# GpSimd subtracts each quarter of a weight unit in four instructions of 256 columns instead of one of 1024

## What is computed

```
x = first_block(x)        # rms norm, projections of x @ w_in (1024 x 9728),
                          # three dilated window attentions, retention in two
                          # directions, gated merge, w_out; then a mixture of 64
                          # experts (group top 1, expert top 2); final rms norm
for l in range(2):        # second_block
    h = rmsnorm(x, g_pre_mix[l])
    y = token_mixer(h, w_in[l], ...)      # mLSTM (4 heads) and window attention (8 heads), w_out
    x = x + rmsnorm(y, g_post_mix[l])
    h = rmsnorm(x, g_pre_ffn[l])
    y = conv_ffn(h, w_up[l], ffn_conv_w[l], w_down[l])   # up to 2 x 2816, conv of 3, gate, down
    x = x + rmsnorm(y, g_post_ffn[l])
```

## Time and profile before

| what | us |
|---|---|
| median of 3 runs (2905.0 to 2905.14) | 2905.1 |
| span of the profiled execution, first to last instruction | 2908.4 |
| TensorE busy | 2679.7 |
| VectorE busy | 1321.1 |
| ACT busy | 873.5 |
| GpSimd busy | 691.6 |

### The profile page before, as it was taken

The page is one execution under the profiler, slowest core; times in us unless marked ns, Lnnn a source line. Parts: engine busy times, 40 slices in busy tenths (PEclk is TensorE's granted clock), DMA queues, the critical chain, the costliest instruction groups (busy, mean ns, idle before and its releaser), DMA issues.

```text
span 2908.4 us, 35516 instructions
## 1 busy us (share of the span) xinstructions
PE 2679.7 (92%) x14188; PEld 1911.4 (66%) x14188; DVE 1321.1 (45%) x2407; ACT 873.5 (30%) x1643; POOL 691.6 (24%) x306
## 2 busy tenths in 40 slices
PE   7999999999988888888888789999999999899998
PEld 7997877888533333333333267788888777788887
DVE  4333745314733333333333367464443564744433
ACT  3333333423211111111111134543333334433332
POOL 4233232542000000000000122224544222144443
PEclk9999999999999999999999989999999999999999
DMA  3222211234999999999999921122232221122321
GB/s 143 87 88 91 91 66 37 102 118 188 380 427 427 428 428 429 429 428 429 429 428 428 382 86 38 50 81 94 87 115 88 85 95 59 58 87 87 94 110 73
DMA packets 126800, 572.19 MB, mean 197 GB/s; under 512 B 10704, under 2 KB 58192, under 8 KB 101328
## 3 DMA queue, kind: packets, MB, share of 16 engines
q1 hardware_dynamic: 121424, 561.08, 48.6%
q10 hardware_dynamic: 5248, 9.32, 1.0%
HBM read 566.12 MB, written 4.26 MB: 196 GB/s over the span
## 4 chain that ended last, share of the span: by engine, by line
PE 63%; DMA 25%; DVE 7%; ACT 3%; issue 1%; POOL 1%; POOLq 0%; SPq 0%; ACTq 0%; DVEq 0%
PE ps L344 39%; DMA wide<-in_moe_w 17%; PE ps L1264 8%; DMA arena<-in_moe_w 6%; PE ps L1692 4%; PE ps L1676 3%; PE ps L569 2%; PE ps L1062 1%; PE ps L540 1%; ACT ring_r L299 1%; PE ps L555 1%; DMA ring<-in_w_in 1%; DMA ring<-in_w_up 1%; POOL ring_r L313 1%; PE ps L1053 1%
## 5 line engine op out<-in xcount | busy, mean ns | idle before, releaser
L313 POOL TENSOR_TENSOR ring_r<-ring,ring_r 128x1024 fp32r<-128x1024 f32 (+1 forms) x280 | 676.7, 2448 | 2138.1 <-ACT ring_r L299 2138.1
L344 PE MATMUL ps<-xnT_r,ring_r 128*128 128x512 f32 (+1 forms) x1664 | 488.2, 376 | 3.4 <-DVE xn_r L2580 2.1
L344 PE MATMUL ps<-ring_r,xnT_r 128*128 128x512 f32 (+1 forms) x1360 | 447.8, 401 | 10.4 <-POOLq L255 5.0
L344 PEld LDWEIGHTS ps<-xnT_r,ring_r 128*128 128x128 f32 x1664 | 306.4, 190 | 63.4 <-POOL ring_r L313 3.4
L344 PE MATMUL ps<-ring_r,arena_r 128*128 128x512 f32 x1392 | 329.3, 394 | 0.0
L344 PEld LDWEIGHTS ps<-ring_r,xnT_r 128*128 128x128 f32 x1360 | 290.9, 226 | 56.4 <-issue 11.6
L344 PE MATMUL ps<-xn_r,ring_r 128*128 128x512 f32 (+1 forms) x832 | 311.9, 375 | 0.0
L344 PEld LDWEIGHTS ps<-ring_r,arena_r 128*128 128x128 f32 x1392 | 261.9, 190 | 58.9 <-issue 4.9
L299 ACT ACTIVATE ring_r<-ring 128x1024 fp32r<-128x1024 f32 (+2 forms) x284 | 270.7, 1024 | 90.2 <-DMA ring<-in_w_down 69.1
L1676 PE MATMUL ps<-wide,arena 128*32 128x512 f32 x1536 | 199.4, 642 | 99.5 <-DMA wide<-in_moe_w 99.0
L1676 PEld LDWEIGHTS ps<-wide,arena 128*32 128x32 f32 x1536 | 42.0, 112 | 236.0 <-DMA wide<-in_moe_w 143.4
(11 more groups left out here) (359 smaller groups left out, 3762.7 us busy)
## 6 DMA issues: line engine op xcount, KB each, us to landing
wide<-in_moe_w SPq DMA_DIRECT2D x144, 2048.0 KB, 27.6
arena<-in_moe_w SPq DMA_DIRECT2D x48, 2048.0 KB, 27.4
ring<-in_w_in SPq DMA_DIRECT2D x25, 2048.0 KB, 8.2
ring<-in_w_up SPq DMA_DIRECT2D x22, 2048.0 KB, 8.6
ring<-in_w_down SPq DMA_DIRECT2D x10, 2048.0 KB, 7.9
ring<-in_w_out SPq DMA_DIRECT2D x6, 2048.0 KB, 8.3
ring<-in_w_ret_branch SPq DMA_DIRECT2D x2, 2048.0 KB, 8.8
attn_spill<-arena ACTq DMA_DIRECT2D x2, 1056.0 KB, 7.3
```

What stands on the lines that cost most here:

```text
L313: nc.gpsimd.tensor_tensor(ring_r[:, q % 2, cols], ring[:, q % 2, cols], ring_r[:, 2 + q % 2, cols].bitcast(F32), ALU.subtract).then_inc(ha ...
L344: ins = nc.tensor.matmul(bank, left, right, start=(start and k == 0), stop=(stop and k == 2))
```

## The change

`low_pool` no longer issues one subtraction for a quarter but four, each over a fourth of its columns (256 of 1024, 132 of 528, 128 of 512). The wait for ACT stays ahead of the first, and only the last counts `half_low` up, so that TensorE waits for the same counts as before.

```diff
+        LOW_PIECES = 4
+
         def low_pool(pool, q):
             if current["l"] is not None and q == Q_UP + 1:
                 pool.wait_ge(half_low, quarter_count(Q_UP, 3))
             for part in range(2 if current["l"] is not None and q == Q_UP else 4):
                 cols = unit_quarter(q, part)
                 pool.wait_ge(half_high, quarter_count(q, part))
-                nc.gpsimd.tensor_tensor(ring_r[:, q % 2, cols], ring[:, q % 2, cols], ring_r[:, 2 + q % 2, cols].bitcast(F32),
-                                        ALU.subtract).then_inc(half_low, 1)
+                n = (cols.stop - cols.start) // LOW_PIECES
+                for at in range(cols.start, cols.stop, n):
+                    piece = slice(at, at + n)
+                    ins = nc.gpsimd.tensor_tensor(ring_r[:, q % 2, piece], ring[:, q % 2, piece], ring_r[:, 2 + q % 2, piece].bitcast(F32),
+                                                  ALU.subtract)
+                ins.then_inc(half_low, 1)
```

## The result

The changed kernel takes 2884.7 us (median of 4 runs) against 2905.05: a ratio of 0.9929, with a 95% interval of 0.9917 to 0.9941. That is 20.4 us faster, where 9 were forecast, and outside the range at its low end (2889). The profiled execution has a span of 2882.5 us, 25.9 less than before. Part of that is the choice of the execution: in every run on record the time is 1.8 to 1.9 us above the span, so the profile of before is of an execution of some 2910.3 us, 5 above its median, and differences between profiles come out that much too large.

The account below looks back on a forecast made before the run. TensorE was busy 92% of the span; by amount GpSimd bounded nothing. TensorE gaps won, -13.0 us, plus 3.4 for late units and 0.4 for the first unit gave -9.2: 2896 us, whole range 2889 to 2923.

Parts of the forecast that it names:

- The price of a piece: GpSimd's 256-column pieces start p = 0.70 us apart, by a line through 1024 and 512 columns; 0.45 us more a quarter.
- VectorE is let in between two pieces: During GpSimd bursts, a two-operand VectorE instruction waits only for the piece in progress: 0.35 to 0.5 us of stall.
- The third rival: Short pieces do not let VectorE in, as the next is already queued: only the cost, +4 us, 2909; chance 0.04.
- What is won is not the stall but TensorE's gap behind it: Attention and mLSTM parts: shorter VectorE stalls remove TensorE's gaps behind them, 3.0 + 2 x 5.0 = 13.0 us.
- the first attention: At 347 to 376 us: shorter VectorE stalls cover TensorE's gaps of 1.44 and 1.81 us but for a rest; 3.0 won.
- In each layer one unit comes late ... 3.4 us: One unit a layer where TensorE waits for GpSimd's quarters and the whole longer burst is exposed: 2 x 1.7 us cost.
- mLSTM: A layer, 1876 to 1894 us: only the first VectorE stall is won, 0.5 us of TensorE's gap of 1.69.
- The rest stage: Rest of the first block: priced at nothing.
- The ends of stages: GpSimd's longer burst before the next stage's opening: nearly nothing at 0.70 us a piece, some 4.4 us at the upper bound.
- The new profile: Expected signs, among them TensorE's wait for the exponentials in 1745 to 1810 falling from 6.3 to about 2 us.
- The up products stay covered: 18 units of up products: the longer GpSimd burst still ends in time, with 0.2 us of cover, costing nothing.
- The rival: Up products wait on GpSimd's fourth quarter once pieces start 0.71 us apart; +18 us, 2923, at 0.78; chance 0.30.

Follow-up runs that it names:

- experiment 8: Two pieces of 512 columns a quarter instead of the change's four, against the kernel before: 2896.4 us, ratio 0.9965.
- experiment 4: Eight pieces of 128 columns a quarter instead of the change's four, against the kernel before: 2972.1 us, ratio 1.0212.
- Experiment 3: Kernel before, GpSimd uncut, with TensorE's four idle times in each layer's window attention filled by transposes nobody reads: 2903.3 us, ratio 0.9986 to the kernel before.
- experiment 2: One instruction for first-block units 0, 11, 12 and each layer's units 3 to 7, four pieces for all others, against the kernel before: 2904.2 us, ratio 0.9999.
- experiment 7: Four pieces only for units 3 and 4 of each layer, which meet the window attention, against the kernel before: 2886.2 us, ratio 0.9932.

## Why the prediction was wrong

- *The price of a piece*: right. p = 0.70 was forecast, 0.69 measured; bursts of 11.2 to 12 us, 11.13 to 12.7 measured for nearly all of 16 pieces of 256 columns (11.64 in the up products, one of 13.26 in the rest stage); a lasting time of 0.73, 0.736 measured. 11.13 - 9.47 = 1.7 us more a burst were measured, which is the line's value. By the 102 cycles a read command of the Trainium skill ("GPSIMD Engine Reference", "Performance pitfalls for Q7 kernels") it would have been 2.0 us, an estimate from that page; the measurement decides.
- *VectorE is let in between two pieces*: right at 256 columns, with 0.67 and 0.74 us and the series of experiment 8, but with exceptions. I had said that L2893 would last 1.4 us at the longest; in the changed kernel (L2899) it lasts 1.24 at the median and twice, at 1937.6 and 2534.9, 2.12 and 2.11, 1.4 over its own 0.69: two further pieces went ahead of it. The third rival does not hold for this change, but at 128 columns it does (experiment 4). No run shows why, nor where between these two sizes it becomes frequent.
- *"What is won is not the stall but TensorE's gap behind it"*: **the step that failed.** As a cap on idle time it held: in layer 0's attention all 6.3 us of waits went (5.6 of them in the stretch above) where I took 4.5, and 2.1 of 3.3 in the first attention where I took 3.0. But I let a microsecond of idle time cost a microsecond. In the kernel before, the idle time of TensorE was followed by half a clock, and in the attention this cost 4.8 us beside the 5.6, a term that my sum had at nothing. Experiment 3 shows that part alone: 4.3 and 4.1 us in the two attentions with every stall in place. The rows were there to read: the same transposes and score products that I had listed around 1763 last up to twice as long after the gap. The clock stood in my own table of stretches too, 0.93 in 1766 to 1810 beside 1.00 in the up products, and I priced nothing by it.
- *"In each layer one unit comes late ... 3.4 us"*: the wait is there (2.4 us against 0.6), the cost is not. It was taken back in the idle times behind it (experiment 2), where I had laid it on the sum. So the errors point the same way: the two attentions gave 18.0 us (9.4 and 8.6 in the table) where the sum had 9.0, mostly by the clock and by some 2 us more of idle time, and a cost of 3.4 wasn't paid. 9.2 + 9.0 + 3.4 is 21.6, where 20.4 were measured. That it comes so near is in part luck, since the terms of the first attention and of the mLSTM can't be told from the clock.
- *The rest stage*, priced at nothing, costs 1.2 us (L1270 waits 0.8 for L318): +1.2 in both kernels of the table with four pieces there, 0.0 in the others. The ends of stages, at nearly nothing, cost nothing: L350 waits 5.1 us for their openings, 5.0 before.
- *The new profile*: TensorE's wait for the exponentials in the attention fell from 6.3 us to nothing, where I had about 2.
- *The up products stay covered*: right, with 0.7 us of cover and not 0.2. TensorE is busy 343.00 of 343 us there, as before. The rival was sound in its place and mechanism, and wrong at its point (0.71; nearer 0.73 by my estimate). Experiment 4 shows it in force.
- *The first attention*: TensorE's gaps fell from 1.44 and 1.81 to 0.50 and 0.64, near the forecast. What this brought can't be told from the clock, as the table shows; the 3.0 us are neither shown nor refuted.

That the clock was lowered by these idle times in particular is shown for the attentions. How much of the rest (mLSTM, starts of stages) is clock or idle time stays open; between two profiles of one kernel such a part differs by up to 6 us.

## What to carry to other kernels

In these traces a GpSimd instruction with SBUF operands is a wall for VectorE's two-operand work of its own length, however small that work is: where such bursts run beside a chain of short VectorE steps, cut the GpSimd instructions to some 0.7 us, at 0.14 us a cut, as long as the burst keeps its deadline. Don't go on to 0.4 us: there VectorE stood for many pieces in a row. And never price TensorE's idle time by its length alone: read the granted clock of the stretch behind it, and add what the matmuls there lose. Read two profiles of one kernel before you explain a few microseconds by the clock.

## What the runs showed of the hardware

- The fixed cost of a GpSimd subtraction in a row of them is 0.14 to 0.15 us from 1024 down to 128 columns: start to start 2.35, 1.25, 0.69, 0.42 us at 1024, 512, 256, 128.
- Between subtractions of 1024, 512 and 256 columns VectorE is let in, mostly at the first end that comes. Between subtractions of 128 columns it can stand far longer: a step of 0.16 us lasted 6.95, past 16 of them.
- No one length of idle time lowers the clock, and the runs don't yield the rule. It fell after two of 1.27 and 1.85 us and of 1.38 and 1.07 (before), but also after a single one of 2.35 and a single one of 1.51 (experiment 8). It stayed at 1.00 after a single one of 1.87 (experiment 2), after 0.78 (experiment 7), and after 1.00, 0.91, 0.99 and 0.46 us, all within 9 us at the exposed unit of the changed kernel.
- Which of VectorE's forms is held up: a product or maximum of two operands in SBUF, and also L589, a multiplication of two numbers a partition by a constant, with one operand (2.31 us before).
